# Head norms of a latent-attention layer taken token tile by token tile, and one set of conditioning sums moved behind the last input projection

## Chip, cores and metric

The kernel runs as one program on one core of a Trainium2 chip. The metric is the device time of one execution in microseconds; lower is better. Everything is float32.

## What is computed

A two-layer diffusion trunk over 128 context tokens and 256 latent tokens (384, three tiles of 128). Each layer is modulated by conditioning sums `silu(cond) @ ada_w`, then has a mixer and a routed mixture of 32 experts. The mixer of layer 0 is a gated convolution beside latent attention with 8 heads. The change is in that attention's preparation:

```python
proj = h @ w_in                                  # 1024 glu, 384 q_a, 256 kv_a, 32 k_rope
q = (rms_norm(q_a, g_q) @ w_qb).reshape(b, s, 8, 96)
q = rms_norm(q, qn_g)                            # over the 96 of each head
c_kv = rms_norm(kv_a, g_kv)
kv = (c_kv @ w_kvb).reshape(b, t, 8, 64 + 64)    # k_nope, v
k = rms_norm(concat([k_nope, k_rope], -1), kn_g) # 64 + 32
q, k = rope on the last 32 of each head          # latent tokens only
o = softmax(q @ k.T * 96 ** -0.5) @ v
```

Latent queries read latent keys and 128 more context keys from a cache, so there are four key tiles: 0 is the new context, 1 and 2 latent, 3 the cache.

## The kernel before

Each engine has a hand-written instruction stream; semaphores join them. TensorE does all products and all transposes (a transpose is a matmul against the identity). Its results go to eight PSUM banks in a fixed order that `psum_order` (L147) writes down once for all engines: `opened` (L593) takes the next bank and first waits until the group eight places earlier has been read, `is_filled` and `is_read` (L421 to L425) are the waits on either side. Weights come by SyncE's DMA queue in the order of `weight_order` (L235) into a ring of six 1 MB slots; `free` (L471) waits until the last product that reads a slot has been made.

The stage around the change, in layer 0:

- **Projections** (`even_projections`, L680). Seven blocks of `IN_BLOCKS` (L111): four for the gated convolution, three ("rest") for q_a, kv_a and k_rope. Between blocks TensorE does conditioning sums (`ada_sums`, L635: 32 matmuls at L645) as `ADA_AFTER_BLOCK` (L112) says, and the four column transposes (`ada_columns`, L654) one block later. Sums (1,0), needed only in layer 1, stand after block 5, their columns after block 6, the last one. VectorE meanwhile does convolution taps (L1399), a fixed number per block, five pairs in the last stretch.
- **Latent norm.** ScalarE copies the last block out (L1183), squares (L1192), takes the root (L1202, with a load of a function table); VectorE takes the reciprocal (L1732) and scales q_a (L1734) and kv_a (L1737). TensorE transposes q_a (three groups of three, L616) and the four kv tiles (two groups of four); ScalarE and VectorE (L1746) copy them out.
- **Query products**, column half by column half: half 0 for tiles 0, 1, 2, then half 1 (three matmuls of 384 columns each, L607). VectorE copies each out (L1750). Then **key and value products**, tiles 0 to 3, two halves each.
- **Query norm** (`head_norm`, L1404, and `head_std`, L1086), once for all three tiles, 2304 elements per partition: ScalarE squares (L1088), VectorE sums (L1408), ScalarE roots (L1090), VectorE reciprocal (L1411), multiplication by it, multiplication by the gain (both L1334).
- **Key norm**, per tile: ScalarE copies keys and values out (L1220, L1221) and squares (L1226), VectorE sums (L1766), ScalarE roots (L1213), VectorE reciprocal (L1759) and two multiplications over 768 elements (L1334).
- **Rope** on GpSimd (L1812 to L1821, six operations on 128 elements): query tiles 1 and 2, then key tiles 1 and 2.
- **Turned heads** (`turned_heads`, L726): TensorE transposes the queries (24, copied by ScalarE at L1246) when `q_ready` comes, the keys (32, copied by VectorE at L1787) when `k_ready` and all key norms have come. Attention (L739) starts after the last copy of both.

Attention of layer 0 has the remaining taps and five more conditioning sums woven in. Its weights, and those behind it, are loaded as ring slots come free.

## Time and profile before

| | |
|---|---|
| time, median of 3 runs | 1214.12 us (1214.08 to 1215.33) |
| the profiled execution | 1215.41 us, span of the profile 1213.5 us |
| mean granted TensorE clock | 0.951 of full |
| TensorE matmul busy | 1103.8 us (91%) |
| VectorE, ScalarE, GpSimd busy | 555.4 (46%), 328.2 (27%), 162.9 us (13%) |
| HBM traffic | 248 GB/s over the span |

The span is the time from the first to the last instruction of the profiled execution; that execution's own time is 1.9 us more, and 1.3 us above the median. Matmul busy time says how long TensorE had matmuls in flight, not that it was at its peak. Times in rows are microseconds from the span's start; L numbers are lines of the kernel before. PE is TensorE, PEld its weight loads, DVE VectorE, ACT ScalarE, POOL GpSimd, SP SyncE; a "q" behind a name is the engine's queue. "[2.25 <-ACT ...]" is idle time before an instruction and what ended it. A granted clock of 1.00 is 2.4 GHz, 0.50 is 1.2 GHz.

### The profile page before, as it was taken

To read this page: it belongs to the slowest core of one execution; us is meant where nothing else is said; L and a number is where in the kernel's file an instruction comes from. 1 tells how busy PE (TensorE), PEld (TensorE's weight loads), DVE (VectorE), ACT (ScalarE), POOL (GpSimd) and SP (SyncE) were. 2 spreads that over 40 slices of the span, in tenths; PEclk is the share of its full clock that TensorE was granted. 3 is DMA by queue.
4 is the path that set the end of the run, shared out by engine and by line. 5 is a ranking of instruction groups with operands and counts; after the bars stand their busy time and mean duration, and the time that the engine had idled before them with its cause. 6 is when DMAs were issued, how large, how long until landed. Compare 5 with 4: busy or idle time off the path is not lost.

```text
span 1213.5 us, 17490 instructions
## 1 busy us (share of the span) xinstructions
PE 1103.8 (91%) x6242; PEld 686.7 (57%) x6242; DVE 555.4 (46%) x1370; ACT 328.2 (27%) x795; POOL 162.9 (13%) x192
## 2 busy tenths in 40 slices
PE   5999868999389999999989999998947999999998
PEld 3456635655255555555548888776534555555554
DVE  2089576521623545445450314784161354454545
ACT  3121253531422122121240111664042221212222
POOL 0400150000410111101010045000040111011100
PEclk8999889999689999999989999998967999999999
DMA  9999616763369999999873223100225999999992
GB/s 354 250 364 332 216 68 226 268 234 104 117 250 422 361 377 375 370 365 375 310 236 99 95 97 119 51 2 5 100 93 220 411 385 365 380 361 371 375 361 89
DMA packets 76712, 301.96 MB, mean 249 GB/s; under 512 B 5540, under 2 KB 34448, under 8 KB 52080
## 3 DMA queue, kind: packets, MB, share of 16 engines
q1 hardware_dynamic: 73392, 291.03, 64.2%
q0 software_dynamic: 2832, 8.61, 2.4%
q10 hardware_dynamic: 432, 1.57, 0.3%
q8 instruction: 36, 0.59, 0.2%
q14 instruction: 20, 0.16, 0.0%
HBM read 291.87 MB, written 9.32 MB: 248 GB/s over the span
## 4 chain that ended last, share of the span: by engine, by line
PE 84%; DVE 5%; ACT 3%; DMA 3%; POOL 2%; issue 2%; SPq 1%; POOLq 0%; DVEq 0%; ACTq 0%
PE banks L607 29%; PE banks L897 18%; PE banks L935 14%; PE banks L919 10%; PE banks L616 5%; PE banks L645 3%; PE banks L908 2%; DVE a L1334 1%; DMA ring<-in_ev_w_in_dram 1%; DVE rt L1334 1%; POOL sorted_rows L1904 1%; PE banks L875 1%; DMA sorted_rows<-a,idx_sorted 1%; DVE xT L1430 1%; DMA a<-sorted_rows 1%
## 5 line engine op out<-in xcount | busy, mean ns | idle before, releaser
L897 PE MATMUL banks<-ring,a 128*64 128x256 f32 x1984 | 228.2, 383 | 5.1 <-POOL a L1916 5.1
L897 PEld LDWEIGHTS banks<-ring,a 128*64 128x64 f32 x1984 | 147.1, 138 | 101.0 <-issue 39.4
L1430 DVE SCALAR_TENSOR_TENSOR xT<-banks,mod,xT 128x128 f32<-128x128 f32 (+1 forms) x512 | 172.3, 410 | 39.7 <-PE banks L935 38.8
L935 PE MATMUL banks<-a 128*128 128x384 f32 x512 | 182.3, 499 | 3.0 <-ACT a L1125 2.6
L607 PE MATMUL banks<-ring,hT 128*128 128x256 f32 (+1 forms) x720 | 154.1, 377 | 3.4 <-DMA ring<-in_ev_w_in_dram 1.9
L1334 DVE TENSOR_TENSOR a<-a,banks 64x256 f32<-64x256 f32 x64 | 27.1, 423 | 270.0 <-ACT a L1110 270.0
L607 PEld LDWEIGHTS banks<-ring,hT 128*128 128x128 f32 x720 | 135.0, 192 | 23.8 <-issue 3.5
L607 PE MATMUL banks<-hT,ring 128*128 128x384 f32 x384 | 127.9, 493 | 1.6 <-ACT hT L1077 1.6
L935 PEld LDWEIGHTS banks<-a 128*128 128x128 f32 x512 | 91.8, 189 | 61.1 <-ACT a L1125 4.3
L919 PE MATMUL banks<-ring,a 128*64 128x512 f32 x512 | 124.0, 605 | 1.7 <-issue 1.2
L1916 POOL COPY a<-a 128x512 f32 x62 | 61.9, 999 | 461.6 <-PE banks L897 418.3
L1124 ACT ACTIVATE a<-banks 64x512 f32<-64x512 f32 x64 | 37.7, 589 | 271.2 <-PE banks L919 271.2
L607 PEld LDWEIGHTS banks<-hT,ring 128*128 128x128 f32 x384 | 73.0, 192 | 53.6 <-issue 3.8
L616 PE MATMUL banks<-ident,a 128*128 128x128 f32 (+1 forms) x294 | 47.3, 332 | 40.1 <-POOL a L1821 10.8
L919 PEld LDWEIGHTS banks<-ring,a 128*64 128x64 f32 x512 | 31.4, 136 | 71.2 <-issue 71.2
L616 PEld LDWEIGHTS banks<-ident,a 128*128 128x128 f32 (+1 forms) x294 | 42.9, 184 | 45.8 <-issue 12.8
L1110 ACT ACTIVATE a<-banks 64x256 f32<-64x256 f32 x64 | 24.1, 377 | 157.5 <-PE banks L897 149.2
L1399 DVE SCALAR_TENSOR_TENSOR a<-a,cols 128x399 f32<-128x399 f32 x120 | 66.3, 626 | 0.0
L1256 ACT ACTIVATE pbuf<-banks,negmax 128x384 f32<-128x384 f32 (+1 forms) x72 | 36.2, 507 | 50.2 <-DVE negmax L1440 49.6
L607 PE MATMUL banks<-a,pTbuf 128*128 128x128 f32 (+1 forms) x336 | 45.0, 275 | 4.6 <-ACT pTbuf L1265 4.4
L1896 POOL TENSOR_TENSOR a<-xT,std 128x384 f32<-128x384 f32 x14 | 14.8, 1089 | 253.8 <-ACT std L1061 253.8
L1420 DVE SCALAR_TENSOR_TENSOR xT<-banks,mod,xT 128x128 f32<-128x128 f32 (+1 forms) x32 | 11.9, 413 | 77.6 <-PE banks L607 77.6
(214 smaller groups left out, 1048.6 us busy)
## 6 DMA issues: line engine op xcount, KB each, us to landing
ring<-in_moe_w_gate_dram SPq DMA_DIRECT2D x64, 1024.0 KB, 6.4
ring<-in_moe_w_up_dram SPq DMA_DIRECT2D x64, 1024.0 KB, 8.7
ring<-in_moe_w_down_dram SPq DMA_DIRECT2D x64, 1024.0 KB, 7.2
ring<-in_ada_w_dram SPq DMA_DIRECT2D x44, 1024.0 KB, 8.1
ring<-in_od_w_qkv_dram SPq DMA_DIRECT2D x12, 1024.0 KB, 5.2
ring<-in_ev_w_in_dram SPq DMA_DIRECT2D x6, 1024.0 KB, 12.8
a<-sorted_rows SPq DMA_DIRECT2D x12, 512.0 KB, 6.4
a<-in_ada_w_dram SPq DMA_DIRECT2D x4, 1024.0 KB, 17.3
```

The source lines that it names most:

```text
L607: mm = pe.matmul(out, lhsT, rhs, start=(k == 0), stop=(k == len(pairs) - 1))
L616: mm = pe.transpose(out[0:w, column:column + r], part, ident[0:r, 0:r])
L645: mm = pe.matmul(out[q:q + 32, :], condS[:, k + odd, :], w[:, odd, 512 * half:512 * half + 512], start=(k == 0), stop=(k == KD - 2), tile_ ...
L897: mm = pe.matmul(bank[1][ROWS * k:ROWS * k + ROWS, 0:FF], teT[n % BUFFERS][:, c, :], w[k][:, c, :], start=(c == 0), stop=(c == KD - 1), ti ...
L919: mm = pe.matmul(bank[3][ROWS * b:ROWS * b + ROWS, :], hidT[:, n % BUFFERS, j, :], slot(i)[:, D * j + 512 * b:D * j + 512 * b + 512], star ...
L935: mm = pe.matmul(bank[4 + 2 * (r % 2) + i][:, 0:TOK], y_pair[q % BUFFERS][:, P * (2 * r + i):P * (2 * r + i + 1)], weights_at[q % BUFFERS] ...
L1124: act.activation(y_pair[n // 2 % BUFFERS][rows, 0:512], bank[3][0:ROWS, :], ACT.Copy)
L1256: done(act.activation(pbuf[:, u % 4, 0:n], psum(("S", l, u))[:, 0:n], ACT.Exp, bias=negmax[:, u:u + 1], accum_out=rowsum[:, u:u + 1]))
L1334: return ve.tensor_tensor(out=out, in0=a, in1=b, op=op)
L1399: ins = ve.scalar_tensor_tensor(out=conv_acc[:, j, :], in0=src, scalar=w, in1=conv_acc[:, j, :], op0=ALU.mult, op1=ALU.add)
L1430: ins = ve.scalar_tensor_tensor(out=xT[:, c, a:b], in0=bank[pair + k][:, a:b], scalar=mcol(l, 5, c, j), in1=xT[:, c, a:b], op0=ALU.mult, o ...
L1916: pool.tensor_copy(teT[n % BUFFERS], sortedT[:, :, bass.ds(first, ROWS)]).then_inc(sem("rowsT_ready"), 1)
```

## The change

- Sums (1,0) go behind block 6 (`ADA_LATE`), their four column transposes between the q_a and the kv transposes, and VectorE's two additions for them in front of its copies of the k_rope part. ScalarE copies the sums after the root of the latent norm. The weights of block 6 are loaded ahead of the pieces of the sums.
- Query products go tile by tile, both halves of a tile together. Squares, sums, roots and norms follow per tile: VectorE copies the next tile's halves between the sum and the norm of a tile; ScalarE takes the root of a tile after the square of the next.
- Key tiles go in the order 1, 2, 0, 3 (`KEY_TILES`); ScalarE squares a tile's keys before it copies its values; VectorE sums and norms one tile after another.
- The gain multiplication over all 96 elements becomes one over the last 32 of each head. The gain of the first 64 is turned into a column once (six small VectorE operations) and multiplied in by the copies of the turned heads, for which 1.0 stands in the other 32 rows.
- Rope waits per tile for the query norm (`q_normed`) and in the new order for the key norm. Layer 1's head norms only shift their index by one (left out below).

```diff
+KEY_TILES = (1, 2, 0, 3)
...
-ADA_AFTER_BLOCK = {1: (0, 2), 2: (0, 3), 3: (0, 4), 4: (0, 5), 5: (1, 0)}
+ADA_AFTER_BLOCK = {1: (0, 2), 2: (0, 3), 3: (0, 4), 4: (0, 5), 6: (1, 0)}
+ADA_LATE = ADA_AFTER_BLOCK[len(IN_BLOCKS) - 1]
...
                 g.add(("qanT", j), "s")
+            g.add(("adaT",) + ADA_LATE, "v")
             for j in range(2):
                 g.add(("ckvT", j), "v")
-            for b in range(2):
-                for t in range(NT):
+            for t in range(NT):
+                for b in range(2):
                     g.add(("q", b, t), "v")
-            for t in range(NT + 1):
+            for t in KEY_TILES:
                 for b in range(2):
...
-            out.append((("w_kvb",), ("kv", 3, 1)))
+            out.append((("w_kvb",), ("kv", KEY_TILES[-1], 1)))
...
                 for j in range(3):
                     turn(opened(("qanT", j)), [proj[:, t, P * j:P * j + P] for t in range(NT)])
+                ada_columns(*ADA_LATE)
                 pe.wait_ge(sem("ckv_normed"), NT)
                 pe.wait_ge(sem("cache_loaded"), 32)
                 for j in range(2):
                     turn(opened(("ckvT", j)), [ckv[:, t, P * j:P * j + P] for t in range(4)])
                 is_read(pe, ("qanT", 2))
-                for b in range(2):
-                    w = arrived("w_qb", b)[:, 0:3 * 384].rearrange("p (k n) -> p k n", k=3)
-                    for t in range(NT):
+                w_q = [arrived("w_qb", b)[:, 0:3 * 384].rearrange("p (k n) -> p k n", k=3) for b in range(2)]
+                for t in range(NT):
+                    for b in range(2):
                         product(opened(("q", b, t))[:, 0:384],
-                                [(qanT[:, k, tile(t)], w[:, k, :]) for k in range(3)], True)
+                                [(qanT[:, k, tile(t)], w_q[b][:, k, :]) for k in range(3)], True)
                 is_read(pe, ("ckvT", 1))
                 w = arrived("w_kvb").rearrange("p (k n) -> p k n", k=2)
-                for t in range(NT + 1):
+                for t in KEY_TILES:
                     for b in range(2):
...
                 pe.wait_ge(sem("q_ready"), l + 1)
+                if l == 0:
+                    pe.wait_ge(sem("q_normed"), NT)
...
-                        if i in ADA_AFTER_BLOCK:
+                        if i in ADA_AFTER_BLOCK and ADA_AFTER_BLOCK[i] != ADA_LATE:
                             ada_copy(*ADA_AFTER_BLOCK[i])
                     act.wait_ge(sem("scalar_step"), step[0])
                     act.activation(small[:, 7, 0:2 * NT], small[:, 6, 0:2 * NT], ACT.Sqrt, bias=eps[:, 0:1]).then_inc(sem("latent_std"), 1)
+                    ada_copy(*ADA_LATE)
                     for j in range(3):
                         is_filled(act, ("qanT", j))
                         done(act.activation(qanT[:, j, :], psum(("qanT", j))[:, 0:TOK], ACT.Identity, scale=col(C_QRG + j)))
-                    is_read(act, ("q", 1, 2))
-                    head_std(l, 0, q_e.rearrange("p t n -> p (t n)"), NT * HEADS, QK)
+                    n = HEADS * QK
+
+                    def head_root(i, row, t, asked, given):
+
+                        act.wait_ge(sem(asked), i + 1)
+                        part = slice(HEADS * t, HEADS * t + HEADS)
+                        act.activation(small[:, row + 1, part], small[:, row, part], ACT.Sqrt,
+                                       scale=1.0 / QK, bias=eps[:, 0:1]).then_inc(sem(given), 1)
+
+                    for t in range(NT):
+                        is_read(act, ("q", 1, t))
+                        act.activation(scratch[:, n * t:n * t + n], q_e[:, t, :], ACT.Square).then_inc(sem("q_squares"), 1)
+                        if t:
+                            head_root(t - 1, 0, t - 1, "q_sums", "q_stds")
                     act.wait_ge(sem("pad_stored"), 16)
                     act.wait_ge(sem("k_rope_placed"), 4)
-
-                    def key_std(t):
-                        act.wait_ge(sem("k_sums"), t + 1)
-                        act.activation(small[:, 3, HEADS * t:HEADS * t + HEADS], small[:, 2, HEADS * t:HEADS * t + HEADS], ACT.Sqrt,
-                                       scale=1.0 / QK, bias=eps[:, 0:1]).then_inc(sem("k_stds"), 1)
-
-                    for t in range(NT + 1):
+                    for i, t in enumerate(KEY_TILES):
                         for b in range(2):
                             is_filled(act, ("kv", t, b))
-                            src = psum(("kv", t, b)).rearrange("p (h e) -> p h e", h=4)
-                            act.activation(k_e[:, t, 4 * b:4 * b + 4, 0:NOPE], src[:, :, 0:NOPE], ACT.Copy)
+                            mark(act.activation(k_e[:, t, 4 * b:4 * b + 4, 0:NOPE], psum(("kv", t, b)).rearrange("p (h e) -> p h e", h=4)[:, :, 0:NOPE],
+                                                ACT.Copy))
+                        if i == 0:
+                            head_root(NT - 1, 0, NT - 1, "q_sums", "q_stds")
+                        act.wait_ge(sem("scalar_step"), step[0])
+                        if i < NT:
+                            act.wait_ge(sem("q_sums"), i + 1)
+                        at = n * (i % NT)
+                        if i == NT:
+                            act.wait_ge(sem("k_sums"), 1)
+                        act.activation(scratch[:, at:at + n], k_e[:, t, :, :].rearrange("p h e -> p (h e)"), ACT.Square).then_inc(sem("k_squares"), 1)
+                        for b in range(2):
                             done(act.activation(v_e[:, t, 256 * b:256 * b + 256].rearrange("p (h e) -> p h e", h=4),
-                                                src[:, :, NOPE:], ACT.Copy))
-
-                        act.wait_ge(sem("read_by_scalar"), groups.count[groups.at[("kv", t, 1)]])
-                        n = HEADS * QK
-                        act.activation(scratch[:, n * t:n * t + n], k_e[:, t, :, :].rearrange("p h e -> p (h e)"), ACT.Square).then_inc(sem("k_squares"), 1)
-                        if t:
-                            key_std(t - 1)
-                    key_std(NT)
+                                                psum(("kv", t, b)).rearrange("p (h e) -> p h e", h=4)[:, :, NOPE:], ACT.Copy))
+                        head_root(i, 2, t, "k_sums", "k_stds")
...
+                if l == 0:
+                    act.wait_ge(sem("head_gains_ready"), 2)
                 for h in range(HEADS):
                     is_filled(act, ("qT", l, h))
                     n = QK if l == 0 else P
-                    done(act.activation(qT[0:n, h, :], psum(("qT", l, h))[0:n, 0:TOK], ACT.Copy))
+                    if l == 0:
+                        done(act.activation(qT[0:n, h, :], psum(("qT", l, h))[0:n, 0:TOK], ACT.Identity, scale=head_gains[0:n, 0:1]))
+                    else:
+                        done(act.activation(qT[0:n, h, :], psum(("qT", l, h))[0:n, 0:TOK], ACT.Copy))
...
+                    ada_columns(*ADA_LATE)
                     for t in range(4):
                         src = proj[:, t, QR + KVR:REST] if t < NT else krope_c
                         ve.tensor_copy(k_e[:, t, :, NOPE:], src.unsqueeze(1).to_broadcast((P, HEADS, ROPE))).then_inc(sem("k_rope_placed"), 1)
                     for j in range(2):
                         is_filled(ve, ("ckvT", j))
                         done(ve.tensor_copy(ckvT[:, j, :], psum(("ckvT", j))))
-                    for b in range(2):
-                        for t in range(NT):
-                            is_filled(ve, ("q", b, t))
-                            done(ve.tensor_copy(q_e[:, t, 384 * b:384 * b + 384], psum(("q", b, t))[:, 0:384]))
-                    is_read(ve, ("q", 1, 2))
-                    head_norm(0, a1[:, 0:NT * HEADS * QK].rearrange("p (r e) -> p r e", e=QK), NT * HEADS, QK, bc[:, B_QN:B_QN + QK], "heads_normed")
-
-                    gain = bc[:, B_KN:B_KN + QK].unsqueeze(1).to_broadcast((P, HEADS, QK))
-
-                    def keys_normed(t):
-                        ve.wait_ge(sem("k_stds"), t + 1)
-                        r, x = small[:, 3, HEADS * t:HEADS * t + HEADS], k_e[:, t, :, :]
+                    n = HEADS * QK
+
+                    def gains_of_nope(i, at):
+
+                        link(scaled(scratch[0:QK, 2304 + QK * i:2304 + QK * i + QK], bc[0:QK, at:at + QK], ident[0:QK, 0:QK]))
+                        link(ve.tensor_reduce(out=head_gains[0:QK, i:i + 1], in_=scratch[0:QK, 2304 + QK * i:2304 + QK * i + QK], axis=AX.X, op=ALU.add))
+                        ve.memset(head_gains[NOPE:QK, i:i + 1], 1.0).then_inc(sem("head_gains_ready"), 1)
+
+                    def q_copied(t, b):
+                        is_filled(ve, ("q", b, t))
+                        done(ve.tensor_copy(q_e[:, t, 384 * b:384 * b + 384], psum(("q", b, t))[:, 0:384]))
+
+                    def tile_sums(i, at, row, t, squares, summed):
+                        ve.wait_ge(sem(squares), i + 1)
+                        ve.tensor_reduce(out=small[:, row, HEADS * t:HEADS * t + HEADS], in_=scratch[:, at:at + n].rearrange("p (r e) -> p r e", e=QK),
+                                         axis=AX.X, op=ALU.add).then_inc(sem(summed), 1)
+
+                    def tile_normed(i, x, row, t, gain, given, ready):
+                        ve.wait_ge(sem(given), i + 1)
+                        r = small[:, row + 1, HEADS * t:HEADS * t + HEADS]
                         link(ve.reciprocal(r, r))
                         link(scaled(x, x, over(r, QK)))
-                        scaled(x, x, gain).then_inc(sem("k_normed"), 1)
-
-                    for t in range(NT + 1):
-                        ve.wait_ge(sem("k_squares"), t + 1)
-                        n = HEADS * QK
-                        ve.tensor_reduce(out=small[:, 2, HEADS * t:HEADS * t + HEADS], in_=scratch[:, n * t:n * t + n].rearrange("p (r e) -> p r e", e=QK),
-                                         axis=AX.X, op=ALU.add).then_inc(sem("k_sums"), 1)
-                        if t:
-                            keys_normed(t - 1)
-                    keys_normed(NT)
+                        scaled(x[:, :, NOPE:], x[:, :, NOPE:], bc[:, gain + NOPE:gain + QK].unsqueeze(1).to_broadcast((P, HEADS, ROPE))).then_inc(sem(ready), 1)
+
+                    def q_normed(t):
+                        tile_normed(t, q_e[:, t, :].rearrange("p (h e) -> p h e", h=HEADS), 0, t, B_QN, "q_stds", "q_normed")
+
+                    gains_of_nope(0, B_QN)
+                    gains_of_nope(1, B_KN)
+                    q_copied(0, 0)
+                    q_copied(0, 1)
+                    for t in range(NT):
+                        if t + 1 < NT:
+                            q_copied(t + 1, 0)
+                        tile_sums(t, n * t, 0, t, "q_squares", "q_sums")
+                        if t + 1 < NT:
+                            q_copied(t + 1, 1)
+                        q_normed(t)
+                    for i, t in enumerate(KEY_TILES):
+                        tile_sums(i, n * (i % NT), 2, t, "k_squares", "k_sums")
+                        tile_normed(i, k_e[:, t, :, :], 2, t, B_KN, "k_stds", "k_normed")
...
-                    done(ve.tensor_copy(kT[0:n, h, :], psum(("kT", l, h))[0:n, :]))
+                    if l == 0:
+                        done(ve.tensor_scalar(kT[0:n, h, :], psum(("kT", l, h))[0:n, :], head_gains[0:n, 1:2], None, ALU.mult))
+                    else:
+                        done(ve.tensor_copy(kT[0:n, h, :], psum(("kT", l, h))[0:n, :]))
...
-                    for buf, normed, ready in ((a1, "heads_normed", "q_ready"), (a2, "k_normed", "k_ready")):
+                    for buf, normed, ready in ((a1, "q_normed", "q_ready"), (a2, "k_normed", "k_ready")):
                         for t in (1, 2):
-                            pool.wait_ge(sem(normed), 1 if buf is a1 else t + 1)
+                            pool.wait_ge(sem(normed), t + 1 if buf is a1 else KEY_TILES.index(t) + 1)
```

## Rows read from the trace of the kernel before

**Rows 1.** Chain that ended last, in order of time, joins: start us, us, what

```profile
119.07 3.57 PE banks L645 x32
122.64 6.73 PE banks L607 x48
...
129.40 0.31 ACT a L1183
...
131.06 1.28 ACT L1202
...
134.14 3.89 PE banks L616 x17
138.03 12.35 PE banks L607 x36
...
250.99 1.53 PE banks L616 x12
```

**Rows 2.** The same chain from the last query copy to the first scores

```profile
150.40 0.57 DVE a L1750
...
162.08 0.46 POOL a L1816
...
166.34 0.46 POOL a L1816
...
170.62 1.05 POOL a L1816
...
176.21 0.46 POOL a L1816
...
179.15 5.92 PE banks L616 x32
...
186.27 0.78 PE banks L607 x3
```

**Rows 3.** Windows: stretch, length, busy us by engine, granted clock, DMA share, GB/s

```profile
129.80:132.50 2.70, 0.00 (x0) 0.00 (x0) 0.66 (x5) 2.67 (x8) 0.00 (x0) 1.00 1.01 401
132.60:139.20 6.60, 5.06 (x20) 4.45 (x21) 4.65 (x13) 1.79 (x4) 4.09 (x5) 0.50 0.66 240
139.40:164.00 24.60, 24.60 (x66) 12.19 (x65) 13.29 (x14) 7.42 (x17) 2.63 (x6) 1.00 0.31 96
```

**Rows 4.** Timeline of VectorE, 124 to 133 us: start us, us, instruction

```profile
129.90 0.17 DVE L1334 TENSOR_TENSOR mod<-banks,cols 128x16 f32<-128x16 f32 x1
...
130.19 0.15 DVE L1334 TENSOR_TENSOR lam<-lam 128x1 f32<-128x1 f32 x1
130.37 0.15 DVE L1729 TENSOR_SCALAR lam<-lam 128x1 f32<-128x1 f32 x1
132.78 0.19 DVE L1732 RECIPROCAL small<-small 128x6 f32<-128x6 f32 x1 [2.25 <-ACT small L1202]
```

**Rows 5.** Instructions by shape, VectorE 128 to 187, ScalarE 118 to 187 us

```profile
L1787 DVE COPY a<-banks 96x512 f32<-96x512 f32 x8 | 5.2, 683 | 6.2 <-PE banks L616 6.1
...
L1334 DVE TENSOR_TENSOR a<-a,small 128x768 f32<-128x768 f32 x4 | 4.2, 1052 | 0.1
L1766 DVE TENSOR_REDUCE small<-a 128x8 f32<-128x768 f32 x4 | 3.7, 942 | 0.0
...
L1737 DVE SCALAR_TENSOR_TENSOR a<-a,small,bc 128x256 f32<-128x256 f32 x3 | 1.3, 480 | 0.0
L1734 DVE TENSOR_SCALAR a<-a,small 128x384 f32<-128x384 f32 x3 | 1.1, 417 | 0.0
...
L1226 ACT ACTIVATE a<-a 128x768 f32<-128x768 f32 x4 | 3.4, 843 | 0.1
L1220 ACT ACTIVATE a<-banks 128x256 f32<-128x256 f32 x8 | 3.0, 373 | 0.0
L1213 ACT ACTIVATE small<-small,eps 128x8 f32<-128x8 f32 x4 | 1.2, 292 | 5.0 <-DVE small L1766 5.0
```

**Rows 6.** DMA issues: form, KB each, median us from issue to landing

```profile
ring<-in_ev_w_kvb_dram SPq DMA_DIRECT2D x1, 1024.0 KB, 6.0
```

More of the change, by code:

```diff
@@ L331, in hybrid_trunk @@
         row_iota = sb("row_iota", [P, 1], I32)
+        head_gains = small[:, 4, 0:2]
         further_code = lam[:, 7:8]
@@ L1241, in _ @@
                             buf = (q_o if b == 4 else k_o[:, 0:NT, :]).rearrange("p t n -> p (t n)")
-                            head_std(l, b // 4, buf, NT * 2 * HEADS, DK)
+                            head_std(l, b // 4 - 1, buf, NT * 2 * HEADS, DK)
+                if l == 0:
+                    act.wait_ge(sem("head_gains_ready"), 2)
                 for h in range(HEADS):
@@ L1782, in _ @@
                             is_read(ve, ("qkv", b - 1, 1))
-                            head_norm(b // 4, buf.rearrange("p (r e) -> p r e", e=DK), NT * 2 * HEADS, DK, bc[:, gain:gain + DK], "heads_normed")
+                            head_norm(b // 4 - 1, buf.rearrange("p (r e) -> p r e", e=DK), NT * 2 * HEADS, DK, bc[:, gain:gain + DK], "heads_normed")
                 for h in range(HEADS):
@@ L1881, in _ @@
                     for i, (buf, ready) in enumerate(((q_o, "q_ready"), (k_o, "k_ready"))):
-                        pool.wait_ge(sem("heads_normed"), i + 2)
+                        pool.wait_ge(sem("heads_normed"), i + 1)
                         if i == 1:
```

## The prediction

> **What bounds the kernel now.** I read the chain of waits in order of time first, for the stretch from the input projections to the first attention scores of layer 0. It has three parts. Up to 129.4 us TensorE works without a gap, and the last thing it does there is the conditioning sums (1,0), 3.57 us, the last projection block (6.73 us) and its transposes [rows 1]. Then TensorE waits: ScalarE copies the last projection tile out at 129.40, squares, loads a function table (1.28 us) and takes the root, and only at 134.14 can the transposes of the normed latents begin [rows 1]. The query products follow to 150.38 and, off the chain, the key and value products. The third part is the one to look at: from 150.40 to 179.15 nothing on the chain is TensorE. One square, one sum and two multiplications over all three query tiles at once run one after the other, then GpSimd turns (rope) query tiles 1 and 2 and key tiles 1 and 2, four rounds that start at 162.08, 166.34, 170.62 and 176.21 and end with the start of the key transposes at 179.15 [rows 2]. Attention starts at 186.27.
>
> Then I read the granted clock by windows: 1.00 in the first 2.7 us of the hole before 134.14, 0.50 from 132.6 to 139.2, 1.00 from 139.4 to 164 [rows 3]. So the 17 latent transposes and the first query products run at 1.2 GHz. VectorE's own timeline shows that it finishes conv taps and small work at 130.52 and then waits for ScalarE's root [rows 4]. Last, the groups by shape give the price of each operation [rows 5].
>
> **Step A, the join.** The sums leave the place before block 6, so the last projection tile is ready 3.57 us earlier, at 125.8, and the root at 129.1 instead of 132.66. But VectorE isn't there: its taps run to 129.9 as before. What it no longer does is the columns of (1,0), from 129.90 to 130.19, so its lambda work ends at 130.52 - 0.29 = 130.2, and the reciprocal starts there instead of at 132.78 [rows 4]: 2.5 us gained, not 3.57. TensorE does the sums from 125.8 to 129.4, in what was its hole, and takes up the latent transposes at 134.14 - 2.5 = 131.6. The four column transposes now stand between the two groups of latent transposes, on the path: 4 x 0.128 = 0.5 us by the twelve at full clock, 4 x 0.229 = 0.9 us by the seventeen at half [rows 1]. ScalarE's copy of the sums sits in its wait for transposes; VectorE's column additions and the new gain vectors (six small operations, at 0.17 us like the 16-wide ones, some 1.2 us with their links) sit in front of the first query copies, which have 12.35 / 6 = 2.1 us of product time for each 0.57 us of copy, and cost nothing; without that cover they would cost their 1.7 us.
>
> The clock decides the rest of this step. The hole shrinks from 4.3 to 2.2 us, less than the 2.7 us that TensorE stood before the clock fell [rows 3]. If it stays up, 17 transposes take 2.2 us instead of 3.89 [rows 1] (1.7 gained), and the 1.3 us of query products at half clock (138.03 to about 139.3) give back 0.65. The last query product, 150.38 now, then ends between 150.38 - 2.5 + 0.5 - 1.7 - 0.65 = 146.0 and 150.38 - 2.5 + 0.9 = 148.8. Neither row is nearer (the hole is shorter than the 2.7 us, but where the fall comes doesn't start with the hole), so I take the middle, **147.4**.
>
> Weights: w_in block 6 is now loaded ahead of the sums' pieces; w_kvb waits for the sums' slots, so it is issued at 129.4, not when those sums ended at 122.6, lands 6.0 us later [rows 6], and is wanted at 147.4. The second w_qb piece, issued at 125.8, has the same 6 us before 136. Both cost nothing.
>
> **Step B, the head of the query chain.** With products tile by tile, squares, sums and norms of tiles 0 and 1 hide under the products of tile 2, except that the root of tile 1 is queued behind the square of tile 2 on ScalarE. After the last product: copy 0.57 [rows 2], square 0.84, root 0.29, reciprocal 0.19 and the gap behind it, 0.23, multiplication 1.05 where GpSimd is in its way and here, where it isn't, 1.0, gain on 8 x 32 elements. That last one no row shows: 0.17 (16 wide) and 0.48 (256 wide, three operands) bound it; I take 0.43, near the latter [rows 4, 5]. With 0.1 of handoffs that is 3.5 us, so query tile 1 is normed at 147.4 + 3.5 = 150.9 and GpSimd starts 11.2 us earlier than 162.08.
>
> **Step C, the two chains behind it.** VectorE and ScalarE then go round for query tile 2 and four key tiles: sum 0.94, root 0.29, reciprocal 0.23, multiplication 1.05, gain 0.43, handoffs 0.1, together 3.05 us [rows 5]. Five times is 15.2: the last key tile is normed at 166.2. GpSimd does four rounds. The last one before, with VectorE idle, took 2.94 us; the first two, in each of which two operations met a VectorE multiplication, 4.27; the third, with four such meetings, 5.59 [rows 2]. So a meeting costs 0.67. In the new order one of the two multiplications per VectorE round is only 0.43 long and can cost no more: 2.94 + 0.67 + 0.3 = 3.9 per round, 15.6 for four, 150.9 + 15.6 = **166.5**. That is the later of the two, by little. It was 179.15: 12.6 us gained.
>
> **Step D, to attention.** Key transposes and their copies took 7.1 us, from 179.15 to 186.27, at VectorE's pace [rows 2]. The copy becomes a multiplication by a gain per partition. From SBUF such a one took 0.417 for 384 elements, by which 512 would take 0.54, and TensorE would set the pace: 0.5 us less. The copies from PSUM took 0.683 [rows 5]; this one reads PSUM, so I take 7.1 unchanged. (The Trainium skill, VectorE: DVE Perf Modes, Mode 2x_2P, says that PSUM has one read port, so the doubled rate is for SBUF alone; by it the sum stays, and no row shows this operation from PSUM.) The query transposes hide: the key products took 13.6 us, 150.4 to 164.0 [rows 3], so TensorE is free of them at 161.0. Everything behind shifts as one: the loads of attention wait for slots, not for a time.
>
> **Sum:** 12.6 us. The profiled execution took 1215.41 (span 1213.5); it becomes 1202.8, and the median of the runs, 1.3 below it, goes from 1214.1 to **1201.5**. Layer 1 only has its index shifted: nothing.
>
> **Rivals.**
> 1. *GpSimd is blocked more.* For it: the whole rope now lies under VectorE's work, and an operation that meets a two-input multiplication takes over twice its time, as the third round shows. With 5.59 per round, 150.9 + 22.4 = 173.3, saving 5.8: 1208.3. Against: only 1.4 of 3.05 us of VectorE's round is multiplications, against 2.1 before. (The Trainium skill, SBUF — State Buffer, Who interferes with whom, says that a VectorE instruction with two SBUF inputs and a GpSimd one that reads SBUF exclude each other for its whole length; the third round agrees.)
> 2. *The clock stays up.* Last product at 146.0, and the norm chain rather than GpSimd the bound: 164.7, saving 14.4: 1199.7.
> 3. *ScalarE becomes the bound.* Per key tile it has four copies of 0.37, a square of 0.84 and a root of 0.29: 2.7 us with gaps, under 3.05 [rows 5], but in a fixed order, and a copy or square that comes late holds the norm. At 0.5 us per tile: 2 us less saving, 1203.5. I count this with the forecast.
> 4. *The time comes back.* Attention would have to wait for weights that aren't sooner. Against: its ring slots are freed by products that all move. It would end at no change, 1214.
> 5. *Slower.* The place is GpSimd's four rounds. 150.9 + 4r reaches 179.15 at r = 7.05 us, that is where every one of the six operations meets a multiplication (2.94 + 6 x 0.67 = 6.96), not one and a half of them. If each sat out a whole multiplication of 1.05 and then took its own 0.46 and a gap, r would be 9.3, the end 188.1, 9 us slower: 1223. Against: VectorE's multiplications don't fill even half of its round.
>
> **How the numbers follow.** Forecast with rival 3 (saving 9 to 14): 0.68. Rival 2: 0.10. Rival 1: 0.15. Rival 4: 0.04. Rival 5: 0.03. The range runs from the clock and PSUM bounds together, 14.4 + 0.5, and 0.7 of the 1.5 us that six gain operations at their lower bound would give (1198.5), to rival 1 with the last product at 148.8 (saving 4.4, 1209.7). A change of 0.2%, 2.4 us, is about what a measurement of this kernel can tell from none: faster by more 0.93, within 0.04, slower 0.03.
>
> **What would show it.** Right: sums (1,0) run inside the former hole; the reciprocal follows the lambda work at about 130.3 with no wait for ScalarE; first rope operation near 151, rounds of 3.9, key transposes near 166.5, attention near 173.7, and the stretches behind it of unchanged length. Wrong: a wait of TensorE for weights at the query products; rope rounds of 5 us; ScalarE's copies as the releaser of VectorE's sums; a later stage that has grown.

## The result, and the profile after

The changed kernel takes 1204.0 us in the median of five runs (1198.5 to 1206.0), the one before 1214.1 (1212.9 to 1215.3). The ratio is 0.9912, 95% interval 0.9885 to 0.9939: 10.7 us less, with 7.4 to 14.0 as the bounds (the ratio is that of the means; the medians lie 10.1 apart). Forecast were 12.6 us less, 1201.5, range 1198.5 to 1209.7. The profiled execution took 1204.0, span 1202.2 against 1213.5. In this execution VectorE ran 0.8 us earlier before the change begins to act (its column additions of sums (0,5) start at 123.35; they started at 124.16). VectorE sets the join, so 0.8 has to be added to the times behind it before they are held against the forecast; I call this the opening of an execution.

The chain of waits after, in order of time, from the join to the first scores (it answers to [rows 1, 2]):

```profile
123.73 5.44 DVE a L1424 x10
...
129.46 0.20 DVE small L1757
...
130.82 1.20 PE banks L622 x9
132.02 0.77 PE banks L660 x4
132.80 1.71 PE banks L622 x8
134.50 8.26 PE banks L613 x24
...
143.38 0.84 ACT a L1227
144.22 0.20 ACT small L1222
...
147.43 0.47 DVE a L1783
...
164.72 1.97 ACT a L1269 x4
...
166.74 5.02 PE banks L622 x32
...
173.69 1.75 PE banks L613 x6
```

Two things are to be seen. The join is now a chain of VectorE: taps (L1424), lambda work, reciprocal, with no wait for ScalarE in it. And GpSimd is gone from the chain altogether; from 147.43 to 164.5 it is VectorE and ScalarE's small roots, round after round. The row at 164.72, four of ScalarE's copies of turned queries, is the profile's guess at the last step, because the fourth copy ended at 166.69. But the first key transpose needs only the first of these copies (the bank eight groups earlier) and the last key norm, which ended on VectorE at 166.63. In the kernel without rope (experiment 11) the transposes start at 164.65, 0.1 us behind the last norm as here, and before ScalarE's fourth copy is done. So I read the norm as the end of the chain. One round, and the last but one, of VectorE's timeline (start, us, instruction, idle before and releaser):

```profile
150.56 0.94 DVE L1787 TENSOR_REDUCE small<-a 128x8 f32<-128x768 f32 x1
151.88 0.20 DVE L1793 RECIPROCAL small<-small 128x8 f32<-128x8 f32 x1 [0.37 <-ACT small L1222]
152.12 1.26 DVE L1359 TENSOR_TENSOR a<-a,small 128x768 f32<-128x768 f32 x1
153.41 0.56 DVE L1359 TENSOR_TENSOR a<-a,bc 128x256 f32<-128x256 f32 x1
...
161.75 1.27 DVE L1359 TENSOR_TENSOR a<-a,small 128x768 f32<-128x768 f32 x1
163.05 0.56 DVE L1359 TENSOR_TENSOR a<-a,bc 128x256 f32<-128x256 f32 x1
```

GpSimd's four rounds start 3.6 to 3.75 us apart; the last one's last operation meets a multiplication (GpSimd's timeline):

```profile
150.73 0.46 POOL L1862 TENSOR_TENSOR a<-a,rope 128x128 f32<-128x128 f32 x1 [14.19 <-DVE a L1359]
...
154.36 0.46 POOL L1862 TENSOR_TENSOR a<-a,rope 128x128 f32<-128x128 f32 x1
...
158.00 0.46 POOL L1862 TENSOR_TENSOR a<-a,rope 128x128 f32<-128x128 f32 x1
...
161.75 0.46 POOL L1862 TENSOR_TENSOR a<-a,rope 128x128 f32<-128x128 f32 x1
...
165.08 1.27 POOL L1867 TENSOR_TENSOR a<-a 128x128 f32<-128x128 f32 x1
```

The clock, by windows (stretch, length, busy us of PE, PEld, DVE, ACT, POOL, granted clock, DMA share, GB/s; it answers to [rows 3]):

```profile
127.90:131.90 4.00, 1.17 (x14) 1.08 (x11) 3.90 (x12) 1.09 (x3) 0.11 (x1) 1.00 0.68 218
132.10:135.30 3.20, 3.20 (x14) 2.87 (x13) 2.33 (x7) 0.83 (x2) 3.20 (x5) 0.50 1.02 381
135.50:160.00 24.50, 24.50 (x67) 12.50 (x66) 17.71 (x33) 9.37 (x23) 9.68 (x17) 1.00 0.58 184
173.69:200.10 26.41, 23.35 (x155) 13.63 (x156) 15.85 (x45) 10.26 (x33) 0.00 (x0) 1.00 0.70 264
200.30:203.50 3.20, 3.20 (x13) 2.49 (x12) 1.26 (x5) 2.13 (x7) 0.00 (x0) 0.50 0.98 389
203.70:241.50 37.80, 35.84 (x268) 22.29 (x268) 17.90 (x59) 18.08 (x49) 0.00 (x0) 1.00 0.78 274
```

It still falls in the join, but only for the 3.4 us from 132.0, where it was down from 132.5 to 139.3. It falls around the turned heads too, in both kernels: from 166.1 to 169.5 here, and before from 166.7 to 173.5 and once more under the key transposes:

```profile
176.90:183.70 6.80, 4.55 (x22) 4.26 (x23) 2.76 (x5) 0.00 (x0) 1.96 (x5) 0.50 0.00 0
```

And it falls at 200.2, in the middle of attention, where the kernel before had it up from 183.7 on.

By stage, in the profiled executions. C is the start of the last query copy, K the first key transpose, S the first scores, M the first of the 66 matmuls of the mixer's output that stand as one piece in the chain, all in us:

| kernel | C | K | S | M | K - C | S - K | M - S |
|---|---|---|---|---|---|---|---|
| before | 150.40 | 179.15 | 186.27 | 253.60 | 28.75 | 7.12 | 67.33 |
| before, again | 150.40 | 179.15 | 186.31 | 253.65 | 28.75 | 7.16 | 67.34 |
| full change | 147.34 | 166.74 | 173.69 | 242.31 | 19.40 | 6.95 | 68.62 |
| full change, again | 148.77 | 168.04 | 174.99 | 244.88 | 19.27 | 6.95 | 69.89 |

So the first scores come 12.6 us earlier, and attention then takes 1.3 us longer; behind it the two executions run in step to within 0.5 us. Of the 11.3 us of span, 0.8 is the opening, 11.8 the change, minus 1.3 in attention.

### The profile page after: what moved, and what is told of

Same layout as the page of the kernel before. It is cut to its first block, busy times and chain, and to the rows that moved or that the text cites. A ratio compares the mean times of both kernels' runs of the same rounds, so it can differ in the third digit from the quotient of the medians.

```text
span 1202.2 us, 17512 instructions
## 1 busy us (share of the span) xinstructions
PE 1103.2 (92%) x6242; PEld 687.0 (57%) x6242; DVE 556.0 (46%) x1384; ACT 329.2 (27%) x799; POOL 156.0 (13%) x192
## 4 chain that ended last, share of the span: by engine, by line
PE 80%; DVE 11%; ACT 3%; DMA 2%; issue 2%; POOL 1%; SPq 0%; POOLq 0%; DVEq 0%; ACTq 0%
PE banks L613 26%; PE banks L906 18%; PE banks L944 14%; PE banks L928 10%; DVE a L1424 5%; PE banks L622 5%; PE banks L651 2%; PE banks L917 2%; DVE a L1359 2%; DVE rt L1359 1%; POOL sorted_rows L1950 1%; PE banks L884 1%; DMA ring<-in_ada_w_dram 1%; DVE xT L1455 1%; DMA sorted_rows<-a,idx_sorted 1%
## 5 line engine op out<-in xcount | busy, mean ns | idle before, releaser
L1962 POOL COPY a<-a 128x512 f32 x62 | 56.8, 917 | 466.5 <-PE banks L906 423.4
L622 PE MATMUL banks<-ident,a 128*128 128x128 f32 (+1 forms) x294 | 44.5, 317 | 30.0 <-DMA a<-in_ev_conv_b_dram 8.8
L1424 DVE SCALAR_TENSOR_TENSOR a<-a,cols 128x399 f32<-128x399 f32 x120 | 66.3, 626 | 0.0
L622 PEld LDWEIGHTS banks<-ident,a 128*128 128x128 f32 (+1 forms) x294 | 40.1, 176 | 36.4 <-issue 13.4
```

Source lines behind the costliest of these rows:

```text
L622: mm = pe.transpose(out[0:w, column:column + r], part, ident[0:r, 0:r])
L1424: ins = ve.scalar_tensor_tensor(out=conv_acc[:, j, :], in0=src, scalar=w, in1=conv_acc[:, j, :], op0=ALU.mult, op1=ALU.add)
L1962: pool.tensor_copy(teT[n % BUFFERS], sortedT[:, :, bass.ds(first, ROWS)]).then_inc(sem("rowsT_ready"), 1)
```

## The experiments

Each ratio is to the kernel before on the same chip, with its 95% interval. The last one ran once, with a profile.

**1. The moved sums alone.** To the kernel before:

```diff
-ADA_AFTER_BLOCK = {1: (0, 2), 2: (0, 3), 3: (0, 4), 4: (0, 5), 5: (1, 0)}
+ADA_AFTER_BLOCK = {1: (0, 2), 2: (0, 3), 3: (0, 4), 4: (0, 5), 6: (1, 0)}
+ADA_LATE = ADA_AFTER_BLOCK[len(IN_BLOCKS) - 1]
...
+                ada_columns(*ADA_LATE)
                 pe.wait_ge(sem("ckv_normed"), NT)
```

> Only the move of sums (1,0) behind the last projection block; norms as before. Theory A (the join is bound by VectorE's taps): the latent transposes start 2.5 us earlier relative to the taps, the last query product 2.3 us earlier, rope rounds as before, attention 2.3 us earlier, time 1211.8. Rival (the sums only change places with the hole and the clock stays low for longer, or the later chain absorbs it): the same time as before within 1 us, 1214.

Median 1213.1 against 1214.4, ratio 0.9989 (0.9977 to 1.0). Its VectorE timeline has the join as expected, a reciprocal that follows the lambda work and waits for nothing, where the kernel before waited 2.25 us for ScalarE [rows 4]:

```profile
130.53 0.15 DVE L1733 TENSOR_SCALAR lam<-lam 128x1 f32<-128x1 f32 x1
130.72 0.19 DVE L1736 RECIPROCAL small<-small 128x6 f32<-128x6 f32 x1
```

C is 147.92, 2.5 us earlier than before (2.9 with the opening, 0.4 later here: 124.60 for the column additions), and K - C is 28.74, untouched. S is 183.17, 3.1 us earlier. The 0.6 between the two is S - K, 6.51 here: the clock was at 1.2 GHz for 3.4 us of the key transposes and not for 6.8, and nothing in this edit reaches there. That execution took 1212.1, which is 1.0 below its own median, while both profiled executions of the kernel before (1215.4 and 1215.0) lie above theirs. So the stage shows 2.5 to 2.9 us, expected were 2.3, and the medians 1.3; the runs of either kernel spread over 5 to 6 us, and the interval leaves 0 to 2.8. The size of this part is known from one profile, not from the medians.

**2. The norms alone.** The full change with `5: (1, 0)` again and the four `ADA_LATE` calls out.

> Tile-by-tile norms, with sums (1,0) where they were. Theory A (the two parts add): the query products end as before (150.4), first rope 3.4 us later at 153.8, key transposes at 169.8, attention 9.5 to 10 us earlier than before, time 1204.4 to 1205. Rival (the parts overlap, one hides the other): within 1 us of the full change.

Median 1205.9, ratio 0.9929 (0.9911 to 0.9946). C 150.27, K 169.55, S 176.49: 9.8 us earlier than before at S, with K - C = 19.28. Do the parts add? The plain sum at S, 3.1 and 9.8, is 12.9, where the full change showed 12.6 and 11.3, but 0.6 of it is the clock in experiment 1, and the openings differ. By stage it is clearer. Behind C the norms alone give 9.5 us and the full change 9.4. Up to C the sums give 2.9, the norms cost 0.5 (0.1 gained, but ScalarE's last copy, which opens this join, started at 128.80 and not at 129.40), and the full change shows 2.3, all with their openings. So they add within 0.2 us. M - S is 69.85: this kernel too lost 2.5 us in attention.

**3. The gain over all 96 elements again.**

```diff
-                        scaled(x[:, :, NOPE:], x[:, :, NOPE:], bc[:, gain + NOPE:gain + QK].unsqueeze(1).to_broadcast((P, HEADS, ROPE))).then_inc(sem(ready), 1)
+                        scaled(x, x, bc[:, gain:gain + QK].unsqueeze(1).to_broadcast((P, HEADS, QK))).then_inc(sem(ready), 1)
```

and plain copies of the turned heads.

> The change, but with the gain multiplied over all 96 elements as before and plain copies of the turned heads. Theory A (the norm chain on VectorE ends last): five norms behind the first rope, each 0.55 to 0.65 us longer, so key transposes 3.2 us later (and 0.5 more from the first norm), 1207.7. Rival (GpSimd's rope ends last, and a longer second multiplication blocks it more): rounds go from 3.6 back to 4.3 us, key transposes 2.0 to 2.8 us later. If neither ends last the time stays at 1204.

Median 1208.8, ratio 0.9952 (0.9937 to 0.9967), 3.3 to 4.8 us above the full change. C 148.99, K 171.58: 22.6 where the full change has 19.3 to 19.4. The chain has only VectorE and ScalarE between them; GpSimd's first round starts at 152.91, its last at 165.53, 4.2 us apart. The norm chain is the bound. The fold of the gain is worth 3.2 of the 9.4 us that the new norms bring up to K. Its copies of the turned keys cost 0.4 of that again: S - K is 6.58 with plain copies, 6.95 with the multiplying ones. From C to S the fold is worth 2.8 to 2.9.

**4. Key tiles in the order 0, 1, 2, 3.** One line, `KEY_TILES = (0, 1, 2, 3)`.

> The change with key tiles in the order 0, 1, 2, 3. Theory A: the norm chain is as long; GpSimd must wait for key tile 1 until about 160.3 (it took it at 158.0), so its last round ends about 167.7, 1.0 us later than now: 1205. Rival (GpSimd is the bound, with no slack at all): the whole wait of 2.3 us comes through, 1206.3.

Median 1205.4, ratio 0.9923 (0.9907 to 0.9938). GpSimd's timeline and the chain show the wait that was expected, and GpSimd at the end of the chain:

```profile
162.73 0.46 POOL L1862 TENSOR_TENSOR a<-a,rope 128x128 f32<-128x128 f32 x1 [2.18 <-DVE a L1359]
...
170.25 6.30 PE banks L622 x32
```

From the first rope (153.37) to K it is 16.9 us, 16.0 in the full change: 0.9 us more, near theory A's 1.0 and far from the rival's 2.3. GpSimd waits 2.2 us, but its last two rounds then meet less of VectorE's work and take 7.5 us instead of 8.4, and part of the wait was slack against the norm chain. So GpSimd is not the bound of the full change, but it is close under it. This profile had no fall of the clock in attention (M - S is 67.35), so its time beside the full change's says nothing on the order.

**5, 6 and 7. Each chain relieved alone, then both.** Sums a tile ahead (the fifth kernel):

```diff
                     for i, t in enumerate(KEY_TILES):
                         tile_sums(i, n * (i % NT), 2, t, "k_squares", "k_sums")
-                        tile_normed(i, k_e[:, t, :, :], 2, t, B_KN, "k_stds", "k_normed")
+                        if i:
+                            tile_normed(i - 1, k_e[:, KEY_TILES[i - 1], :, :], 2, KEY_TILES[i - 1], B_KN, "k_stds", "k_normed")
+                    tile_normed(NT, k_e[:, KEY_TILES[NT], :, :], 2, KEY_TILES[NT], B_KN, "k_stds", "k_normed")
```

with ScalarE's root moved behind its next square. Query tiles in the order 1, 2, 0 (the sixth): the same lists with `QUERY_TILES = (1, 2, 0)` in place of `range(NT)` in the products, copies, squares and norms. The seventh has both.

> The changed kernel once more, beside the variants built on it. Both theories: 1204 within 1.5 us, key transposes 19.4 us after the last query copy begins. Where TensorE's clock falls in the join and in attention may differ from the first profile; with no fall in attention the profiled execution is some 1.3 us shorter.

> The change, with each key tile's sum one tile ahead of the norm before it on VectorE, and its root behind the next square on ScalarE, so the 0.37 us wait for a root is hidden. Theory A (norm chain and GpSimd's rounds end together): the norm chain ends 1.3 us earlier, GpSimd's last round stays at 15.6 us after the first rope, so key transposes gain only 0.3 us: 1203.7. Rival (the norm chain alone is the bound): 1.3 us or more less, 1202.7.

> The change, with query tiles in the order 1, 2, 0, so that GpSimd can begin rope while tile 0's products run. Theory A: first rope 4.5 us earlier relative to the last query copy, GpSimd is done 3 us before the norm chain, which still sets the end: 0 to 0.6 us less (the last norms are met by no rope): 1203.6. Rival (GpSimd is the bound): 2 us or more less.

> Both edits together. Theory A: neither chain covers for the other any longer, and key transposes come 1.5 to 2 us earlier than in the full change, more than the sum of the two alone: 1202. Rival (something else ends last, such as key products or ScalarE's copies): no more than the larger of the two alone.

| kernel | median, ratio (interval) | K - C | S - K | M - S |
|---|---|---|---|---|
| full change, again | 1205.5, 0.9924 (0.991 to 0.9937) | 19.27 | 6.95 | 69.89 |
| sums ahead | 1205.1, 0.9914 (0.9901 to 0.9928) | 19.02 | 6.94 | 69.92 |
| query order | 1204.0, 0.9909 (0.9895 to 0.9924) | 18.43 | 7.10 | 70.03 |
| both | 1203.7, 0.991 (0.9896 to 0.9923) | 18.89 | 7.67 | 67.33 |

The full change itself came at the edge of its 1204 within 1.5. Of the variants, theory A was right for the first (0.25 us less, 0.3 expected) and near for the second (0.84, expected 0 to 0.6, its rival 2 or more). The third is a miss: 0.38, not 1.5 to 2. What stopped it is in VectorE's and ScalarE's timelines of that kernel:

```profile
158.43 0.95 DVE L1790 TENSOR_REDUCE small<-a 128x8 f32<-128x768 f32 x1 [0.92 <-ACT a L1246]
...
161.87 0.95 DVE L1790 TENSOR_REDUCE small<-a 128x8 f32<-128x768 f32 x1 [0.79 <-ACT a L1246]
```

```profile
157.14 0.38 ACT L1236 ACTIVATE a<-banks 128x256 f32<-128x256 f32 x1 [1.16 <-PE banks L614]
...
160.57 0.39 ACT L1236 ACTIVATE a<-banks 128x256 f32<-128x256 f32 x1 [1.16 <-PE banks L614]
```

VectorE waits for ScalarE's square, ScalarE for the second half of the tile's key products, and both recur every 3.43 us: that is TensorE's pace, two halves of two 512-column products. In this order VectorE takes the sum of a tile before the norm of the tile ahead of it, so a square that isn't there holds the norm as well, and each norm comes a tile later. In the order of the full change TensorE's pace isn't the bound: without rope (experiment 11) K - C fell to 17.82, and VectorE waited for roots only, 0.37 us each, never for a square. So TensorE's products are a third chain for sums ahead, and the miss is the price of that edit, not a floor under every version.

**8 and 9. The key copies shared.** Even heads stay with VectorE, odd ones go to ScalarE:

```diff
-            g.add(("kT", l, h), "v")
+            g.add(("kT", l, h), "vs"[h % 2] if l == 0 else "v")
...
+                    act.wait_ge(sem("cache_stored"), 32)
+                    act.wait_ge(sem("k_normed"), NT + 1)
+                    for h in range(1, HEADS, 2):
+                        is_filled(act, ("kT", l, h))
+                        done(act.activation(kT[0:QK, h, :], psum(("kT", l, h))[0:QK, :], ACT.Identity, scale=head_gains[0:QK, 1:2]))
```

alone, and with the query order of the sixth.

> The change, with the copies of the turned keys shared: even heads by VectorE, odd heads by ScalarE (the transposes' 5.0 us, not VectorE's 8 x 0.71, then set the pace). Theory (this stretch is bound by VectorE's copies): from the key transposes to the first scores 5.7 instead of 6.95 us, of which 0.3 goes to ScalarE's later table load: 1 us less than the full change. Rival (ScalarE's own queue, with eight query copies first, is the bound): the same time or up to 0.5 us more.

> Query order 1, 2, 0 and the shared key copies together: 0.8 us from the first and 1.0 from the second, so from the last query copy to the first scores 24.5 us against 26.3 in the full change; time 1.8 us less. Rival: the two meet in ScalarE's queue and give no more than 0.8.

Alone: median 1204.8, ratio 0.9927 (0.9914 to 0.9939), S - K = 7.25, not 5.7: a miss. With the query order: 1203.4, ratio 0.9914 (0.9898 to 0.993), K - C = 18.45, S - K = 5.78, so S - C is 24.2 (24.5 expected). The two differ in the clock under the 32 transposes, by windows of the first and of the second:

```profile
166.30:172.90 6.60, 5.57 (x27) 5.36 (x28) 3.13 (x5) 4.22 (x9) 0.65 (x1) 0.50 0.00 0
```

```profile
165.60:168.80 3.20, 2.54 (x12) 2.42 (x13) 1.27 (x3) 3.12 (x7) 0.00 (x0) 0.50 0.01 4
```

With VectorE out of the way TensorE sets the pace, and its pace is that of the clock: 6.4 us for the transposes in the first, 5.0 in the second. The second kernel is the best here by its stage, 2.1 us less than the full change from C to S; but its attention took 70.4 us, and by the medians, 1203.4 with an interval that overlaps the full change's, no version was shown to beat it.

**10. The kernel before once more.**

> The kernel before, profiled once more. Theory (TensorE's clock in attention falls or not by where the kernel lies on the clock's own beat, for any version): attention takes 66.6 us with the clock up all through, 67.9 or 69.1 where a stretch at 1.2 GHz falls into it; either may show. Rival (only the changed kernel has the fall): 66.6 and no fall. Median 1214.5 either way.

Median 1214.4, ratio 0.9999 (0.999 to 1.0008). Attention again takes 67.3 us by the measure of the table (66.6 by that of the expectation, which ended 0.8 us earlier), with the clock up throughout:

```profile
186.31:252.90 66.59, 61.23 (x437) 37.66 (x438) 35.03 (x109) 30.96 (x88) 0.00 (x0) 1.00 0.77 280
```

Beside it the full change of the second profile (windows):

```profile
174.99:201.70 26.71, 23.65 (x158) 13.91 (x159) 15.85 (x45) 10.56 (x33) 0.00 (x0) 1.00 0.71 267
201.90:208.50 6.60, 6.60 (x17) 4.08 (x16) 1.35 (x6) 3.46 (x8) 0.00 (x0) 0.50 0.46 183
208.70:244.10 35.40, 33.68 (x263) 21.30 (x262) 17.62 (x58) 16.68 (x47) 0.00 (x0) 1.00 0.82 289
```

So the expectation that any version may show either is not borne out by the kernel before (two profiles, none), nor is the rival: of the versions with the new norms, three (key order, both, the shared copies alone) kept the clock up as well. More under the last heading.

**11. No rope.** The rope operations of layer 0 on GpSimd are taken out.

> The change without the rope operations of layer 0 on GpSimd (queries and keys of the latent tokens stay unturned). Theory (the norm chain sets the end, GpSimd only slows it by meeting its multiplications): each of VectorE's rounds goes from 3.1 to 3.3 down to 2.9 us, key transposes come 17.9 to 18.1 us after the last query copy instead of 19.3. Rival (TensorE's key products, 3.43 us per tile, set the end): 18.6 us or more. If GpSimd set the end: under 17 us.

K - C is 17.82 (17.9 to 18.1 expected; 18.6 or more if TensorE's products set the end). With nobody to meet, VectorE's large multiplication takes 0.96 and the small one 0.42, round after round:

```profile
160.02 0.20 DVE L1793 RECIPROCAL small<-small 128x8 f32<-128x8 f32 x1 [0.37 <-ACT small L1222]
160.25 0.96 DVE L1359 TENSOR_TENSOR a<-a,small 128x768 f32<-128x768 f32 x1
161.25 0.42 DVE L1359 TENSOR_TENSOR a<-a,bc 128x256 f32<-128x256 f32 x1
```

GpSimd's presence thus costs the norm chain 1.5 us from C to K (19.3 to 19.4 with it), 0.3 per round, although GpSimd's own chain isn't the one that ends last. The single run took 1202.1.

## Why the prediction was right, and where it was off

- **Step A, the join: as predicted.** The transposes start at 130.82 + 0.8 = 131.6 (131.6). The reciprocal follows the lambda work at once. The clock did neither of the two bounds: it fell 1.2 us after TensorE had resumed, q_a's nine transposes ran at full (1.20 us), the columns between, kv_a's eight at half (1.71), and it was back by 135.4, before the first query product was done. 134.50 plus 18 products at 1.93 per three (the copies of one tile's halves start that far apart) and 0.54 for the part at half clock (the first four halves took 8.26 where four times 1.93 is 7.72) gives 146.6, with the 0.8 it is 147.4 (147.4). That the number fits to 0.1 is luck: I had taken the middle between two bounds 2.8 us apart. The hole was 2.8 us long, not 2.2, mostly because TensorE ran further ahead of VectorE than in the kernel before (its columns of (0,5) came 1.2 us earlier, VectorE's 0.8).
- **Step B: a wait that I had not seen.** I let the last query copy follow its product. It started at 147.34, 0.7 us after it could, because VectorE was busy: the chain shows the reason in its rows from 143.38 on. ScalarE takes the root of tile 0 only behind the square of tile 1, VectorE waits 1.1 us for it, and so the norm of tile 0, another copy and the sum of tile 1 still stand in front of that copy. I had written that tiles 0 and 1 hide under the products of tile 2; they stick out by 0.7. That is also the 0.5 us that the norms alone lose before C in experiment 2. The head behind the copy took 3.39 us to the first rope (3.5).
- **Step C: right engines, tie the other way.** GpSimd took 3.63, 3.64, 3.75 and 4.6 us for its rounds, 15.6 together (15.6). VectorE took 16.0 for its five (15.2), so the norm chain ended last, by 0.3 us (166.6 against 166.35). Two terms were mis-sized: the multiplication, 1.03 to 1.27 us next to GpSimd where I took 1.05 from [rows 5], 0.4 us in all five, and the 256-wide gain, 0.42 alone as I had guessed, but 0.56 beside GpSimd, 0.7 in all. I had charged GpSimd for each meeting and VectorE for hardly any; experiment 11 gives its charge as 1.5 us.
- **Step D: the number right, the pace not.** S - K is 6.95 (7.1). I had read the stretch before as VectorE's pace. Copy by copy it was that for the second half only: its first five copies start 0.79 to 0.86 us apart, waiting for transposes at 1.2 GHz, the rest 0.60 apart. After, the multiplications (L1831) wait for transposes twice and are 0.66 apart from the third on:

```profile
167.91 5.67 DVE L1831 TENSOR_SCALAR a<-banks,small 96x512 f32<-96x512 f32 x8 [1.27 <-PE banks L622]
```

```profile
L1831 DVE TENSOR_SCALAR a<-banks,small 96x512 f32<-96x512 f32 x8 | 5.5, 741 | 1.4 <-PE banks L622 1.3
```

  The multiplication is thus slower than the copy, 0.741 against 0.683 us each, which two fewer waits for the clock made good: the unchanged 7.1 is in part luck. It isn't the 0.54 that the rate from SBUF would have given. On the Trainium skill's sentence (VectorE: DVE Perf Modes, Mode 2x_2P), that only SBUF operands get the doubled rate, the trace now agrees with a row of its own.
- **"Everything behind shifts as one": the step that failed.** Up to S the forecast is 12.6 and the profile 11.8, or 12.6 if the opening is counted in; attention then gave back 1.3 us in one profile and 2.6 in the other. With it the full change is 10.7 and 9.2 us by the two comparisons. The loads were not the cause: between S and M TensorE waited 0.2 us for one of them, and 3.8 us for ScalarE's copies, against 4.4 before. The clock is: the same 441 matmuls kept TensorE busy for 63.1 us instead of 61.5.
- **Rivals.** Neither 2 nor 5 happened. (The sum of rival 2 was off by 0.4: by its own prices GpSimd's rounds end at 149.5 + 15.6 = 165.1, behind the norm chain's 164.7.) Of 1, GpSimd's blocking, the mechanism was there in the size of the forecast, 3.9 per round and not 5.6, and the other engine paid as well, which I had not priced. Of 3, ScalarE's order, the root behind the next square was the form it took, 0.7 us at the head instead of 0.5 per key tile. Rival 4, that time comes back, came in part and not by the cause I gave it.

## What to carry to other kernels

When a chain over one big tile is cut into pieces, read off how many engines' chains then run side by side and by how little they differ: here 16.0 and 15.6 us. Reordering the work of either, or of both, gave under 1 us, and one reordering ran into a third chain, TensorE's 3.43 us per tile. Taking GpSimd's work away gave 1.5, through VectorE's chain and not its own. An in-order engine that takes piece i's small step behind piece i+1's large one delays the engine that waits for it and all that is queued there. And a gain that can be folded into a copy that is made anyway was worth 2.8 to 2.9 us up to the first scores, a good quarter of what the new norms bring.

## What I had not expected of the hardware

- Where GpSimd and VectorE meet, both pay. VectorE's 768-wide multiplication of two SBUF operands went from 0.96 to as much as 1.27 us, its 256-wide one from 0.42 to 0.56; a GpSimd operation went from 0.46 to between 1.05 and 1.27 beside the wide one. The Trainium skill (SBUF — State Buffer, Who interferes with whom) has two such operations exclude each other for an instruction's length, and one meeting agrees. VectorE's multiplication of 152.12 (1.26 us, shown above) began 0.02 us behind a GpSimd operation and took 0.30 more than alone. The next GpSimd operation began in the middle of it and ended 0.31 us behind it:

```profile
152.10 0.46 POOL L1865 TENSOR_TENSOR a<-a,rope 128x128 f32<-128x128 f32 x1
152.64 1.05 POOL L1866 TENSOR_TENSOR a<-a 128x128 f32<-128x128 f32 x1
```

- The clock under attention. The same instructions took 67.3 to 67.6 us with the clock at 2.4 GHz throughout, 68.6 with one stretch of 3.4 us at 1.2 GHz, and 69.9 to 70.4 with one of 6.8 us. In the seven profiles that have such a stretch (leaving out the kernel without rope, where it came with the first scores) it begins 26.5 to 27.6 us after them, behind a wait of TensorE of 1.5 us for ScalarE's copies, which the kernel before has too, at 212.0, where its clock stayed up. The full change had the fall in both profiles, the kernel before in none of two. What decides it stays open: that the earlier start of attention brings it about isn't shown, since three variants that start attention as early don't have it. One thing separates the thirteen profiles, the stretch at 1.2 GHz around the key transposes. In the six without a fall in attention it ended 1.6 to 2.5 us before the first scores (183.7 against 186.3 before, 173.0 against 174.6 in the shared copies alone). In the seven with a fall the clock was back 3.1 to 4.2 us before them (169.5 against 173.7 in the full change, 168.9 against 172.0 in the best by its stage). No run varied this alone, so it is a mark and not a shown cause. From K to M the best by its stage took 76.2 us and the shared copies alone 74.8, so here the gain at the transposes was gone by the end of attention. The fall is worth up to 2.6 us in the full change, more than any edit tried on top of it, and one profile per version can't say how often it comes.
